# Big products with the moving operand and the bank taken from the last column to the first

## What is computed

```python
def swiglu(h, w_gu, w_down):
    g, u = jnp.split(h @ w_gu, 2, axis=-1)
    return (jax.nn.silu(g) * u) @ w_down

def moe_ffn(h, router, w_gu, w_down):
    ...
    for e in range(N_EXPERTS):
        out = out + gate[..., e:e + 1] * swiglu(h, w_gu[e], w_down[e])
    return out

# mixers:  h @ w_in ... @ w_out
# second block:  proj = jnp.einsum('bsd,de->bse', h, w_in)
```

## Time and profile before

| what | value |
| --- | --- |
| median of 3 runs | 2073.43 us (2073.12 to 2076.48) |
| the profiled execution's own time | 2075.21 us |
| its span in the trace | 2073.4 us |
| mean granted TensorE clock | 0.982 |
| PE busy | 1975.6 us, 95% |
| VectorE busy | 1725.3 us, 83% |
| ScalarE busy | 1328.1 us, 64% |
| DMA | 560.19 MB, mean 270 GB/s |

### The profile page before, as it was taken

How to read it: one execution, slowest core, us unless ns; L and a number is a source line. 1 busy time by engine, 2 the same in 40 slices (tenths; PEclk the granted TensorE clock), 3 DMA queues, 4 the chain that set the end, 5 groups by cost and what they waited for, 6 DMA issues and landing times.

```text
span 2073.4 us, 28446 instructions
## 1 busy us (share of the span) xinstructions
PE 1975.6 (95%) x10316; PEld 1644.3 (79%) x10316; DVE 1725.3 (83%) x2440; ACT 1328.1 (64%) x1977; POOL 0.2 (0%) x4
## 2 busy tenths in 40 slices
PE   6998999989989999999999999999999998999997
PEld 5777889978877788788888878888888876767785
DVE  7798878768776698989989898998989988785764
ACT  4353534355564587788788787888878774554543
POOL 0000000000000000000000000000000000000000
PEclk9999999999999999999999999999999999999999
DMA  9856689846332298999999999999989994672630
GB/s 378 300 170 234 229 301 327 287 142 207 116 111 82 91 382 325 359 334 382 366 351 365 329 368 345 374 352 340 371 325 377 380 354 158 222 247 68 217 122 21
DMA packets 154211, 560.19 MB, mean 270 GB/s; under 512 B 17232, under 2 KB 17488, under 8 KB 153936
## 3 DMA queue, kind: packets, MB, share of 16 engines
q1 hardware_dynamic: 154064, 558.29, 74.1%
HBM read 557.18 MB, written 1.05 MB: 269 GB/s over the span
## 4 chain that ended last, share of the span: by engine, by line
PE 78%; DVE 12%; ACT 5%; issue 3%; DMA 2%; DVEq 0%; SPq 0%; ACTq 0%
PE ps L527 22%; PE ps L529 22%; PE ps L528 22%; PE ps L533 10%; DVE spl L516 3%; PE ps L537 3%; DVE macc L580 2%; ACT sph L504 2%; DMA ring<-in_hyb_w_in 1%; DVE arena L2169 1%; DMA ring<-in_dense_down 1%; ACT arena L771 1%; ACT arena L2135 0%; DVE hL L884 0%; ACT ps L890 0%
## 5 line engine op out<-in xcount | busy, mean ns | idle before, releaser
L504 ACT ACTIVATE sph<-ring 128x1024 fp32r<-128x1024 f32 x906 | 949.2, 1059 | 517.0 <-PE ps L529 332.8
L516 DVE TENSOR_TENSOR spl<-ring,sph 128x1024 fp32r<-128x1024 f32 x906 | 1078.2, 1219 | 241.5 <-ACT sph L504 229.0
L527 PE MATMUL ps<-sph,hH 128*128 128x512 f32 (+1 forms) x1296 | 522.6, 403 | 1.4 <-DVE hL L884 1.3
L529 PE MATMUL ps<-sph,hL 128*128 128x512 f32 (+1 forms) x1296 | 507.8, 392 | 0.0
L528 PE MATMUL ps<-spl,hH 128*128 128x512 f32 (+1 forms) x1296 | 506.9, 391 | 0.0
L529 PEld LDWEIGHTS ps<-sph,hL 128*128 128x128 f32 x1296 | 245.5, 189 | 52.6
L527 PEld LDWEIGHTS ps<-sph,hH 128*128 128x128 f32 x1296 | 246.4, 190 | 51.3 <-issue 3.8
L528 PEld LDWEIGHTS ps<-spl,hH 128*128 128x128 f32 x1296 | 246.4, 190 | 48.4 <-issue 1.0
L527 PE MATMUL ps<-sph,rH 128*128 128x512 f32 x664 | 269.1, 405 | 5.9 <-ACT arena L3123 2.3
L529 PE MATMUL ps<-sph,rL 128*128 128x512 f32 x664 | 259.9, 391 | 0.0
L528 PE MATMUL ps<-spl,rH 128*128 128x512 f32 x664 | 259.4, 391 | 0.0
(11 more groups left out here) (317 smaller groups left out, 1754.4 us busy)
## 6 DMA issues: line engine op xcount, KB each, us to landing
ring<-in_moe_gu SPq DMA_DIRECT2D x448, 512.0 KB, 5.4
ring<-in_moe_down SPq DMA_DIRECT2D x224, 512.0 KB, 5.3
ring<-in_mod SPq DMA_DIRECT2D x144, 512.0 KB, 5.0
ring<-in_w_in SPq DMA_DIRECT2D x64, 512.0 KB, 4.5
ring<-in_dense_gu SPq DMA_DIRECT2D x44, 512.0 KB, 5.3
ring<-in_ssm_w_in SPq DMA_DIRECT2D x40, 512.0 KB, 4.2
ring<-in_dense_down SPq DMA_DIRECT2D x22, 512.0 KB, 5.4
ring<-in_hyb_w_in SPq DMA_DIRECT2D x20, 512.0 KB, 5.9
```

The source lines that it names most:

```text
L504: a.activation(k.high[m % SPLITS][:, 0:w], raw[:, 0:w], ACT.Copy).then_inc(k.S.half_rounded, 1)
L516: v.tensor_tensor(k.low[m % SPLITS][:, 0:w], raw[:, 0:w], k.high[m % SPLITS][:, 0:w], ALU.subtract).then_inc(*k.tick(k.S.half_split, f"hal ...
L527: pe.matmul(out, a[0], b[0], start=start, stop=False, skip_group_check=True)
L529: return pe.matmul(out, a[1], b[0], start=False, stop=stop, skip_group_check=True)
```

## The change

`mm3` turns three views round before it uses them: the output, and the high and the low part of the moving operand. The stationary operand stays. Column n of a product is then still the product with column n of the moving operand, and it is written to the same place; the columns are only gone through from the last to the first. In the program that is built, these operands have the step -1 and start at their last column (for example `[-1,256]` at offset 255, where it was `[1,256]` at offset 0). All callers of `mm3` are reached by it; `mm` and `turn` are not. The instructions, their order and their waits are the same on all engines. The lines after L526 stand one lower in the changed kernel.

```diff
 def mm3(pe, out, a, b, start, stop):
-    pe.matmul(out, a[0], b[0], start=start, stop=False, skip_group_check=True)
-    pe.matmul(out, a[0], b[1], start=False, stop=False, skip_group_check=True)
-    return pe.matmul(out, a[1], b[0], start=False, stop=stop, skip_group_check=True)
+    out, high, low = out[:, ::-1], b[0][:, ::-1], b[1][:, ::-1]
+    pe.matmul(out, a[0], high, start=start, stop=False, skip_group_check=True)
+    pe.matmul(out, a[0], low, start=False, stop=False, skip_group_check=True)
+    return pe.matmul(out, a[1], high, start=False, stop=stop, skip_group_check=True)
```

## The result

The changed kernel takes 2096.22 us (median of four runs, 2088.63 to 2100.25), the kernel before 2074.95 us beside it. The ratio is 1.010, with a 95% interval of 1.0078 to 1.0122: about 21 us slower. The forecast of no change was wrong. The time lies inside the range of 2066 to 2112 us, but only in the part that I had left to the "longer turn", with a chance of 0.09: 2.7 ns for each matmul on average (21.3 us / 7800). It isn't the same addition for both widths, though, and it doesn't come from the side that I held to be the riskier one, the bank.

What follows compares the result with a forecast made beforehand. TensorE, busy for 95% of the span, was taken to bound the kernel. The three terms for reading downwards, writing downwards and the turn summed as 0 + 0 + 0 to a forecast of 2073.4 us, range 2066 to 2112 us.

Steps and rivals of the forecast that it cites:

- forecast of no change: Whole kernel: the time stays at 2073.4 us, within 0.2%; chance 0.69.
- longer turn: Rival, at each matmul's start or end: direction costs a few nanoseconds, mostly 1 to 5 ns, say 2090 us; chance 0.09.
- What bounds the kernel: Whole kernel: TensorE, busy 1975.6 of 2073.4 us, sets the time; a matmul's step goes almost fully into the end time.
- The change adds and moves no instruction: All engines: no instruction, wait or DMA byte added or moved; only the step of two operands of 7800 matmuls differs.
- (a): Moving operand of the helper's matmuls, read downwards: taken as 0, bounds 0 and +0.200 us for 512 columns.
- the half rate: Rival, all helper matmuls: downwards, two columns no longer go together, about 3420 us; chance 0.18.
- (b): Bank of the helper's matmuls, written downwards: taken as 0 with less confidence; upper end +0.200 us at 512 columns, +0.093 at 256.
- (c): Turn from one matmul to the next: taken as 0, within -13.5 to +13.5 ns; each nanosecond worth 7.8 us.
- the bounds of 13.5 ns: Turn between matmuls: time over the columns, same at 512 and 256 columns; hidden gives -13.5 ns, doubled +13.5.
- pairs formed by direction: Column pairs in the array: the forecast is wrong if direction, not place, forms them; half-rate sign 0.43 us at full clock.
- If only one of the two directions has a price: Operand or bank: the page can't tell which has the price; a kernel with only one of them reversed would.
- Giving back: Price of the turn over all 7800 matmuls: 7.8 us, 0.38% of the whole, for each nanosecond.

Runs made afterwards that it cites:

- e_only512: Changed kernel with only the 512-column products downwards, the others upwards as before; against the kernel before: 2099.65 us against 2075.47, ratio 1.0117.
- m4_loads: Small separate kernel of 20 float32r forms, varying the stationary operand's place or columns; upwards 226.7 ns a step, 233.5 with the stationary operand from column 16.
- e_shift: Kernel before, all upwards, with the tile `small` moved behind `rL`, shifting the activations 32 columns modulo 64 against the weights: 2093.98 us against 2075.13, ratio 1.0085.
- m1_widths: Small separate kernel, bank and moving operand each up or down at five widths; 512 columns: 226.7 ns both up or bank down, 233.3 moving down or both down.
- e_moe_bank: Kernel before with experts' weights stored reversed per 512 columns, read upwards, bank written downwards in 4032 matmuls: 2075.33 us, ratio 0.9997.

## Why the prediction was wrong, step by step

*What bounds the kernel*: right. PE sets the time, and the step that is 6.67 ns longer reached the end time to nearly two thirds (24.2 of 38.9 us in e_only512).

*The change adds and moves no instruction*: right, the counts are the same on every engine.

*(a) Reading the moving operand downwards, taken as 0*: this is the step that failed. It measures +6.67 ns at 512 columns and -1.6 ns at 256. The reason given, "the addresses touched are neighbours just as before and the number of columns is the same", is true and doesn't bear the conclusion: the step depends on how the read of the moving operand runs against the stationary one's, and the same columns against a stationary operand at another offset, read upwards, lose 6 to 7 ns too (m4_loads, e_shift). The upper bound, the half rate with +0.200 us, was 30 times too far.

*(b) Writing the bank downwards, taken as 0 with less confidence*: the value was right (m1_widths, e_moe_bank), the doubt misplaced. I had a rule of the Trainium skill ("PSUM — Partial Sum Buffer", section Specifications (TRN2)) to weigh for the bank and none for the operand, and let that decide where the risk was.

*(c) The turn between matmuls, taken as 0, with a price that would be the same for both widths*: the bounds of 13.5 ns held, and the size that I named for the rival, 1 to 5 ns for 7800 matmuls, held as a mean. Its form was wrong: the steady step of 5832 matmuls became 6.7 ns longer and that of 1920 became 1.6 ns shorter. I had taken the 13.5 ns over the columns for a fixed cost because 512 and 256 columns both show it. 384 columns show it too (173.3 - 160 = 13.3), but 192 and 128 columns both take 111.7 ns, and the repeated column 218.7. So what is over the columns isn't a constant of the turn: it changes with the places and the order of the two operands.

*Giving back*: the prediction priced the turn at 7.8 us for each nanosecond, with nothing returned. Had I known the 6.67 ns, the sum would have been +38.9 us for the 512-column products, where e_only512 measured 24.2. I had taken 0.227 us for the step of all of them. Their mean under 300 ns at the full clock is 228.0 ns, and 233.4 in the changed kernel, so the difference is 5.4 ns and not 6.67, some 31 us. The rest is shorter distances around the small products, PE's few waits (0.6 us an expert), and the clock; it isn't split up further.

*The half rate, with a chance of 0.18*: its size exists (451 ns for every second column), and its sign of being wrong, pairs formed by direction, didn't come. A downward read of neighbours stays near the quick rate.

*"If only one of the two directions has a price, a kernel with only the operand or only the bank reversed would tell"*: it did.

What stays open: which reads meet in what way. For 512 columns the runs show the relation (alike modulo 64 columns for offsets in steps of 16, and runs of 64 columns or more). Plain float32 has no price of the direction at 256 columns; its offsets were not run. That it is a clash of two readers in the same memory is argued from this and not shown. The moving operand from column 4 (231.7 ns), the one-column stationary operand (231.1 ns) and the two steps of one and the same 256-column product fit no simple form of it.

## What to carry to other kernels

Keep the moving operand of long float32r matmuls upwards in runs of 64 columns or more; the order of such runs and the direction of the bank are free. For 512 columns let stationary and moving tiles begin alike modulo 64 float32 columns (256 bytes), each at a multiple of 16 columns, and look at the step again whenever a tile's size or place in the allocation changes: one tile moved cost 0.85% here with no line of the products touched. For 256 columns these runs give no rule. Read the step from the starts of a long row of matmuls at the full clock; multiply a difference by the count, and then look how much of a row really runs at that step, since here a row needed some ten matmuls to reach its quick one. Compare two traces only after the distances at the low clock are taken out: they were half of what seemed to be given back.

## What the runs showed of the hardware that I had not expected

- For 512 columns the upward step of 226.67 ns is the good case, not the normal one: most shifts of one operand against the other, and every downward read that was run, take 229 to 237 ns.
- That quick step has to settle: after an interruption about ten steps of 228 to 236 ns come first. Downwards it is one.
- A 256-column product can have two steps, 113.3 or 117.8 ns, and a row keeps the one in which it has settled.
- Reading up and down by turns takes 236.7 ns on average, more than either direction.
- Every second column of a float32r moving operand doubles the step (451 ns for 512 columns); every fourth takes 233.3 ns for 256 columns, where neighbours take 120.
- The step has a floor: 128 columns are no quicker than 192, both take 111.7 ns (stationary operand of 128 columns).
- The bank may be written in either direction at no cost in float32r, and in plain float32 (256 columns) in every second column.
